# Mamba scan written feature by token in one set of matmuls, with the conv features and gates kept in memory chunk by chunk, in a hybrid decoder layer on Trainium2

## The reference, cut to what matters

```python
cum = jnp.cumsum(dtc * a.reshape(g, r), axis=2)
seg = cum[:, :, :, None] - cum[:, :, None, :]
decay = jnp.exp(jnp.where(causal, seg, -jnp.inf))
cb = jnp.einsum('bcign,bcjgn->bcijg', cc, bc)
y_diag = jnp.einsum('bcijgr,bcjgrp->bcigrp', cb[..., None] * decay * dtc[:, :, None], xc)
to_end = jnp.exp(cum[:, :, -1:] - cum) * dtc
states = jnp.einsum('bcjgn,bcjgr,bcjgrp->bcgrpn', bc, to_end, xc)
chunk_decay = jnp.exp(cum[:, :, -1])
...
y_off = jnp.einsum('bcign,bcigr,bcgrpn->bcigrp', cc, jnp.exp(cum), h_prev)
return (y_diag + y_off).reshape(b, s, nh, hp), h_last.reshape(b, nh, hp, D_STATE)
...
y = y + xs.astype(jnp.float32) * d_skip.astype(jnp.float32)[:, None]
y = y.reshape(b, t, D_SSM) * jax.nn.silu(z.astype(jnp.float32))
```

## Time and profile before

| | |
|---|---|
| median of 3 runs | 1902.06 us (1902.06 to 1903.03) |
| the profiled execution's own time | 1900.08 us |
| its span, first to last instruction | 1898.1 us |
| PE busy / DVE / ACT / POOL | 1825.6 / 1418.9 / 900.3 / 1066.2 us |
| mean granted TensorE clock | 0.990 |
| `weave` | about 330 to 789 us of the span |
| `mixers` | about 782 to 1003 us |

### The profile page before, as it was taken

How to read it: one execution, slowest core, us unless ns; L and a number is a source line. 1 busy time by engine, 2 the same in 40 slices (tenths; PEclk the granted TensorE clock), 3 DMA queues, 4 the chain that set the end, 5 groups by cost and what they waited for, 6 DMA issues and landing times.

```text
span 1898.1 us, 33584 instructions
## 1 busy us (share of the span) xinstructions
PE 1825.6 (96%) x12740; PEld 1686.7 (89%) x12740; DVE 1418.9 (75%) x1915; ACT 900.3 (47%) x1680; POOL 1066.2 (56%) x863
## 2 busy tenths in 40 slices
PE   8999999899999999999988999999999999999999
PEld 7999999888888889755557799999999998999999
DVE  5788840698888767589987564897777779787876
ACT  5334422677777778556642012343333344444442
POOL 4588740677756766334443222355555557787774
PEclk9999999999999999989999999999999999999999
DMA  4444442645455442789976524215334366434442
GB/s 175 149 156 176 183 148 75 159 117 124 101 134 120 125 124 90 253 304 322 321 244 214 190 97 186 91 45 205 147 125 165 148 230 254 159 137 147 148 136 92
DMA packets 139097, 309.31 MB, mean 163 GB/s; under 512 B 31659, under 2 KB 65323, under 8 KB 135228
## 3 DMA queue, kind: packets, MB, share of 16 engines
q1 hardware_dynamic: 115356, 271.15, 42.8%
q10 hardware_dynamic: 23584, 36.04, 5.6%
HBM read 222.42 MB, written 93.28 MB: 166 GB/s over the span
## 4 chain that ended last, share of the span: by engine, by line
PE 72%; DVE 13%; issue 6%; DMA 4%; ACT 3%; POOL 2%; SPq 0%; ACTq 0%; DVEq 0%; POOLq 0%
PE ff_ps L2742 32%; PE proj_ps L469 9%; PE dense_ps L1055 6%; PE wo_psa L2577 5%; PE proj_ps L552 3%; PE att_t_ps L1087 2%; PE wo_psb L2709 2%; DVE silu_half L1216 2%; DMA tmp_xbc<-silu_half 1%; PE wo_psa L2709 1%; PE att_s_ps L1073 1%; DVE att_p L1169 1%; PE att_s_ps L1074 1%; PE ssd_in L1773 1%; DVE sa_vlo L2108 1%
## 5 line engine op out<-in xcount | busy, mean ns | idle before, releaser
L2742 PE MATMUL ff_ps<-ff_set,ff_wring 128*128 128x264 f32 x5376 | 661.1, 285 | 11.1 <-DVE ff_set L3355 4.4
L2742 PEld LDWEIGHTS ff_ps<-ff_set,ff_wring 128*128 128x128 f32 x5376 | 658.0, 189 | 13.8 <-DVE ff_set L3355 5.3
L2411 POOL TENSOR_TENSOR ff_wring<-const,ff_wring 128x256 fp32r<-128x256 f32 (+1 forms) x192 | 211.9, 1107 | 148.0 <-ACT ff_wring L2908 147.9
L985 POOL TENSOR_SCALAR att_p<-att_p,att_rden 128x128 f32<-128x128 f32 (+6 forms) x112 | 197.0, 1768 | 117.1 <-DVE att_rden L1147 116.8
L2908 ACT ACTIVATE ff_wring<-const 128x256 fp32r<-128x256 f32 (+1 forms) x192 | 93.6, 489 | 220.4 <-PE ff_ps L2742 116.0
L3377 DVE TENSOR_TENSOR h<-h,ff_ps 128x528 f32<-128x528 f32 x192 | 133.2, 700 | 51.8 <-PE ff_ps L2742 47.2
L1282 ACT ACTIVATE att_pThi<-att_t_ps 128x512 fp32r<-128x512 f32 x192 | 93.2, 487 | 93.7 <-PE att_t_ps L1087 79.4
L1055 PE MATMUL dense_ps<-u_hi,w_hi 128*128 128x352 f32 x480 | 121.8, 335 | 4.7 <-POOL w_lo L254 2.1
L1169 DVE CUSTOM_DVE_ANT_0 att_p<-att_s_ps,att_bias 128x128 f32<-128x128 f32 (+7 forms) x128 | 94.9, 753 | 37.9 <-PE att_s_ps L1074 34.7
L1156 DVE TENSOR_TENSOR att_pTlo<-att_t_ps,att_pThi 128x512 fp32r<-128x512 f32 x192 | 104.5, 551 | 20.5 <-ACT att_pThi L1282 19.8
L1055 PE MATMUL dense_ps<-u_hi,w_lo 128*128 128x352 f32 x480 | 119.4, 330 | 0.0
(11 more groups left out here) (385 smaller groups left out, 4350.8 us busy)
## 6 DMA issues: line engine op xcount, KB each, us to landing
tmp_r_sets<-h SPq DMA_DIRECT2D x16, 1848.0 KB, 6.4
ff_setraw<-tmp_r_sets SPq DMA_DIRECT2D x56, 528.0 KB, 5.4
sa_k<-in_cache_k SPq DMA_DIRECT2D x32, 640.0 KB, 9.1
sa_v<-in_cache_v SPq DMA_DIRECT2D x40, 512.0 KB, 4.6
w_raw<-in_w_feat SPq DMA_DIRECT2D x36, 512.0 KB, 6.3
out_qk<-proj_out SPq DMA_DIRECT2D x16, 528.0 KB, 7.9
tmp_bias_rows<-tmp_table ACTq DMA_DIRECT2D x8, 1024.0 KB
att_bias<-tmp_bias_rows SPq DMA_DIRECT2D x16, 512.0 KB, 3.5
```

Of the source, the lines that this page charges most:

```text
L985: pool.tensor_scalar(slot(h, qt), slot(h, qt), rden[:, qt, :], None, ALU.mult).then_inc(normed, 1)
L2411: pool.tensor_tensor(w_set(n)[:, 1], operand(q, m), w_set(n)[:, 0].bitcast(F32), ALU.subtract).then_inc(fw_split, 1)
L2742: mm = pe.matmul(ff_ps[:, (b + g) * 512:(b + g) * 512 + HG], ws[:, wi, k, :], xs[:, xi, k, g * HG:(g + 1) * HG], start=(opens and k == 0 a ...
```

## The change

1. `store_feat` and `store_last` write the features and gates chunk by chunk: row 128·n + p of `xbc` now holds, for partition p, the 12 tiles' 128 tokens of chunk n (6 KB in a row); `z` likewise with 8 tiles (4 KB). A store of a tile is cut into pieces of 512 B for it (1024 of them), where it was a row of 4 KB for each partition. `load_chunk` and `load_z` read a whole row for each partition, where they gathered 512 B pieces. The samples' columns go to tensors of their own (`xbc_s`, `z_s`), with one more store for each z tile.
2. `inner` is written with x·dt as the weights (64 features of one head), two heads side by side in 64 output partitions each, and the decay matrix as the moving side, so that the result comes out feature by token. The carried state's part is added in the same PSUM tile: the weights are the state, the moving side is `grown` = exp(cum)·C. `off`, `scale_off`, `add_inner` and `turn_y` are gone; `add_skip` reads the product directly, from two PSUM tiles.
3. `grown` is made for each group by ACT (`grow_exp`, an exponential of 128x1024) and POOL (`grow`, a product of 128x1024). It is read from the rows of cum before `segment` overwrites them. The decay of the state is cut in two halves (`decay`). The squares have a buffer of their own (`ssd_sq`).
4. The order of all engines' lists in a pass is rewritten.

```diff
-                    act.dma_start(rows[:, 0:SEQ], half[:, 0:SEQ]).then_inc(feat_stored, 16)
+                    act.dma_start(by_chunk("xbc", d), chunked(half[:, 0:SEQ])).then_inc(feat_stored, 16)
...
-                sp.dma_start(xbc[j][:], dram["xbc"][:, cols].rearrange("(f p) t -> p f t", p=P)).then_inc(loaded[j], 16)
+                if n >= 3:
+                    sp.wait_ge(grown_made, 2 * (n - 2))
+                sp.dma_start(xbc[j][:].rearrange("p f t -> p (f t)"), dram["xbc"][n * P:(n + 1) * P, :]).then_inc(loaded[j], 16)
...
-                for h in range(8 * g, 8 * g + 8):
-                    if h % 4 == 0:
-                        pe.wait_ge(mix_made, 4 * n + h // 4 + 1)
-                    mm = pe.matmul(in_ps[:, (h % 8) * HD:(h % 8 + 1) * HD], mixm[n % 2][:, h, :],
-                                   xdt[:, h * HD:(h + 1) * HD], start=True, stop=True)
+                if n:
+                    pe.wait_ge(y_skipped, 2 * n + g - 1)
+                    pe.wait_ge(grown_made, 2 * n + g - 1)
+                    pe.wait_ge(state_summed, 2 * n + g - 1)
+                for f in range(4):
+                    if f % 2 == 0:
+                        pe.wait_ge(mix_made, 4 * n + 2 * g + f // 2 + 1)
...
+                    for r in range(2):
+                        mm = pe.matmul(out(r), xdt[:, cols(r)], mixm[n % 2][:, 8 * g + 2 * f + r, :], start=True, stop=(n == 0))
+                    if n:
+                        for r in range(2):
+                            mm = pe.matmul(out(r), state[:, cols(r)], grown[g][:, 2 * f + r, :], start=False, stop=True)
...
+            def grow(n, g):
+                pool.wait_ge(grown_exp, 2 * n + g - 1)
+                pool.wait_ge(loaded[n % 2], 16 * (n // 2 + 1))
+                pool.tensor_tensor(grown[g][:], grown[g][:],
+                                   xbc[n % 2][:, KD + 2 + g, :].unsqueeze(1).broadcast_to([P, NH // 2, P]),
+                                   ALU.mult).then_inc(grown_made, 1)
...
+            def grow_exp(n, g):
+                act.wait_ge(rows_loaded[n % 2], 16 * (n // 2 + 1))
+                if n >= 2:
+                    act.wait_ge(in_made, 2 * n + g - 1)
+                act.activation(grown[g][:], mixm[n % 2][:, 8 * g:8 * g + 8, :], ACT.Exp).then_inc(grown_exp, 1)
...
+                if n + 1 < NC:
+                    grow_exp(n + 1, 0)
+                    segment_next(n + 1, 0)
+                    segment_next(n + 1, 1)
                 if n:
                     exponent(n)
                     square(n - 1)
                     keep_probs(n)
```

More of the change, by code:

```diff
@@ L1726, in turn_x @@
                 mm.then_inc(x_turned, 1)
-            def turn_y(n, g):
-                pe.wait_ge(y_summed, 2 * n + g + 1)
-                if 2 * n + g:
-                    pe.wait_ge(y_skipped, 2 * n + g)
-                for f in range(4):
-                    mm = pe.transpose(y_ps[:, f * P:(f + 1) * P], y[n % 2][:, (4 * g + f) * P:(4 * g + f + 1) * P],
-                                      kit.c(C_IDENT, P))
-                mm.then_inc(y_turned, 1)
             def norm_sums(n):
@@ L1744, in norm_sums @@
                 mm.then_inc(normed, 1)
-            def off(n, g):
-                if g:
-                    pe.wait_ge(y_scaled, 2 * n - 1)
-                else:
-                    pe.wait_ge(state_summed, 2 * n)
-                pe.matmul(off_ps[:], xbc[n % 2][:, KD + 2 + g, :], state[:, half(g)], start=True,
-                          stop=True).then_inc(off_made, 1)
-            def states(n, g):
-                if g:
-                    pe.wait_ge(state_summed, 2 * n + 1)
-                else:
-                    if n:
-                        pe.wait_ge(y_scaled, 2 * n)
+            def states(n, g):
+                if 2 * n + g:
+                    pe.wait_ge(state_summed, 2 * n + g)
+                if g == 0:
                     pe.wait_ge(xw_made, n + 1)
@@ L1804, in _ @@
                 if n:
-                    off(n, 0)
-                    turn_y(n - 1, 0)
+                    inner(n, 0)
                     sample_scores(n, 0)
-                    off(n, 1)
                     sample_scores(n, 1)
@@ L1811, in _ @@
                     sample_scores(n, 2)
-                    turn_y(n - 1, 1)
                     sample_scores(n, 3)
-                states(n, 0)
-                inner(n, 0)
-                states(n, 1)
-                if n:
+                    states(n, 0)
+                    inner(n, 1)
+                    if n + 1 < NC:
+                        chunk_start(n + 1)
                     sample_turn(n)
-                inner(n, 1)
+                    states(n, 1)
+                else:
+                    states(n, 0)
+                    inner(n, 0)
+                    states(n, 1)
+                    inner(n, 1)
                 sample_values(n, 0)
-                if n + 1 < NC:
+                if n == 0:
                     chunk_start(n + 1)
-                else:
-                    norm_sums(n - 1)
                 sample_values(n, 1)
@@ L1827, in _ @@
                     turn_x(n + 1, 0)
-                else:
-                    turn_y(n, 0)
                 sample_values(n, 2)
@@ L1922, in _ @@
                     kit.clear(pool)
-            mixed.pool_tail = skip_x, sum_squares
+            mixed.sum_squares = sum_squares
         @block.scalar
@@ L2002, in _ @@
                 if n + 1 < NC:
+                    keep_b(n + 1)
                     cast_v(n, 3)
-                    keep_b(n + 1)
                     cast_v(n, 4)
-                    for q in range(4):
-                        segment(n + 1, q)
+                    grow_exp(n + 1, 1)
+                    segment_next(n + 1, 2)
+                    segment_next(n + 1, 3)
             mixed.act_tail = square, cast_v
@@ L2048, in weigh @@
                                   ALU.mult).then_inc(x_kept, 1)
-            def scale_off(n, g):
-                dve.wait_ge(off_made, 2 * n + g - 1)
-                if g == 0 and n >= 2:
-                    dve.wait_ge(y_turned, 2 * n - 2)
-                dve.tensor_tensor(heads(y[n % 2][:, half(g)]), heads(off_ps[:]), per_head(decays[:, 0, n, 8 * g:8 * g + 8]),
-                                  ALU.mult).then_inc(y_scaled, 1)
             def add_state(n, g):
@@ L2181, in _ @@
                     weigh(n + 1, 1)
-                    keep_own(n)
-                    scale_off(n + 1, 0)
                     mix(n + 1, 0)
@@ L2187, in _ @@
                         keep_norm(n - 1)
-            mixed.dve_tail = keep_own, add_skip, gate, keep_out, keep_norm, split_v
+                    keep_own(n)
+            mixed.dve_tail = keep_own, gate, keep_out, keep_norm, split_v
     return mixed
@@ L2616, in _ @@
                 step(k, (0, 1))
-                if k == 0:
-                    turn_y(last, 1)
                 if k == 1:
@@ L3090, in scale @@
                                          op1=ALU.mult).then_inc(y_scaled, 1)
-            keep_own, add_skip, gate, keep_out, keep_norm, split_v = mixed.dve_tail
+            keep_own, gate, keep_out, keep_norm, split_v = mixed.dve_tail
             last = mixed.chunks - 1
@@ L3098, in _ @@
             split_v(last, 4)
-            add_skip(last, 0)
             keep_own(last)
             split_a(2)
-            add_skip(last, 1)
             gate(last)
```

170 lines of the change are left out of this document (83 added, 87 removed).

## The result

The changed kernel took 1909.73 us (median of 5 runs, 1905.66 to 1911.8) against 1902.06 for the kernel before in the same job: ratio 1.0039, 95% interval 1.0025 to 1.0053. It is slower by 0.39%, about 7.5 us; the forecast was 1898, faster. Its profiled execution has a span of 1909.4 us (before 1898.1) and a mean granted clock of 0.986 (0.990).

What follows compares the result with a forecast made beforehand. Before, DVE was what a 23.74 us pass waits for most; after, late rows of cum would bind at 22.9. Terms -5.1 - 1.3 + 2.8 = -3.6 us from 1902.06 gave 1898.5, given as 1898; 8-in-10 range 1887 to 1910.

Steps and rivals of the forecast that it cites:

- -5.1 for the passes: Loop of `mixers`: six passes each 0.85 us shorter, at 22.9 us, set by late rows of cum; chance 0.32.
- -1.3 for the loop's end: End of the `mixers` loop: an `add_skip` of 0.69 us and a turn of 0.6 leave the chain.
- +2.8 for the stores: `weave`: feature stores in 512 B pieces land 0.7 us later, on the path about four times.
- further falls of the clock: Rival, loop of `mixers`: PE's clock falls more often, 3.5 us each; slower from the third, 1909; chance 0.17.
- dear stores: Rival, `weave`: stores cost their upper bound, 18 us; about 1911; chance 0.10, shared with `inner` products at 4.1 us.
- 10.2 + 3.8 = 14 us, in gaps that are there: POOL in a pass: two added products of 128x1024, 1.91 us each, fit into its idle time.
- DVE's 21.3: DVE's stretches of a pass, 10.66 + 4.45 + 6.18 us; the pass length if rows of cum land in time, chance 0.22.
- about 1.9 us of work: DVE in a pass: two mixes between the last `weigh` and `keep_own`, covering the wait for PE's last value product.
- The rows of cum: Loop from last value product through the rows' load, ACT and softmax to the next: 22.7 to 23.6 us, binding.
- ACT's 4.8: ACT in a pass: one exponential and half the next chunk's `segment` ahead of the softmax's exponentials, 4.8 us.
- A group of `inner` in 16 products: PE in a pass: 2.1 us a group if two products run side by side, 4.1 if not.
- The wait of DVE ahead of `keep_own`: DVE in a pass: its 1.32 us wait for PE's last value product vanishes.

Runs made afterwards that it cites:

- the rows in time: Changed kernel with the rows of cum issued right behind the features, ahead of the values: 1897.1 us, ratio 0.9982 to the kernel before.
- the memsets: Changed kernel, rows of cum loaded ahead of the values, three POOL memsets in place of each `grow` product, state's part left out: 1891.83 us, ratio 0.9954.
- the run with one head of eight: Changed kernel, rows of cum loaded ahead of the values, POOL's product with C made for only one head of eight: 1886.7 us, ratio 0.9935.
- The layout alone: Kernel before with the change's stores and loads of features and gates, and its old mixers: 1902.62 us, ratio 1.0024.
- the run with `skip_x` twice: Kernel before with POOL's product of the skip made twice in each chunk: 1926.45 us, ratio 1.0131.

## Why the prediction was wrong, point by point

The forecast was the sum -5.1 for the passes, -1.3 for the loop's end and +2.8 for the stores. The two profiled spans differ by +11.3: the five middle passes give +7.3 (125.69 us against 118.37), the rest of the loop -1.0, and `weave` +5.2; -0.2 lie behind the loop. The passes are where it failed. That 1909.73 still lies under the 1910 of the range is luck: that end stood for further falls of the clock or for dear stores, and not for a longer pass.

**"POOL gets two products [...] 10.2 + 3.8 = 14 us, in gaps that are there", and with it DVE's 21.3.** This is the step that failed: it priced each engine's list by itself, as if nothing that POOL does could lengthen an instruction of DVE. The gaps were there for POOL's time, but beside DVE's mixes and splits, with which POOL's products exclude each other. In the pass with the rows in time, mixes and splits wait 5.2 us: 2.77 and 2.98 for two pairs of mixes instead of 1.28 (as beside the memsets), and two splits at 2.14 and 2.31 instead of 1.22. Of this, 2.4 stand beside a `grow` (the mixes at 901.00 and the split at 915.53). The other 2.8 stand beside products that POOL made before the change too: the mixes at 921.04 beside `weigh_x`, where the prediction put "about 1.9 us of work" and 2.98 were measured, and the split at 918.20 beside `skip_x`. The kernel before had about 1.1 of such waits already, and showed it:

```profile
895.88 1.87 DVE L2016 TENSOR_TENSOR ssd_m<-ssd_m,ssd_cb 128x512 f32<-128x512 f32 x2
...
898.01 0.68 DVE L2016 TENSOR_TENSOR ssd_m<-ssd_m,ssd_cb 128x512 f32<-128x512 f32 x1
...
899.81 1.19 DVE L2016 TENSOR_TENSOR ssd_m<-ssd_m,ssd_cb 128x512 f32<-128x512 f32 x1
```

```profile
898.02 2.44 POOL L1912 TENSOR_TENSOR ssd_state<-ssd_state,ssd_decays 128x1024 f32<-128x1024 f32 x1 [0.82 <-POOL sa_bias L1863]
```

One mix 0.68, another 1.19, of the same size: the second ends 0.54 us after POOL's decay (898.02 + 2.44 + 0.54 = 901.00). The prediction took the mean of these (0.95 for a mix) as the price of the instruction. With 4.1 us more of waiting, not all of it on the path, 21.3 becomes the measured 24.5. By itself this already makes a pass 0.7 us longer than before. Taking most of the two products away gives back 1.6 of the 3.2 (22.87, the run with one head of eight).

**The rows of cum.** The mechanism was right and its size too small; in the kernel as built this loop is the longer one, so this term failed as well. From the last value product to the landing passed 8.3 us (904.34 to 912.64; forecast 6.1 to 7.0). The prediction took the landing down from the 8.2 us of the earlier trace rows, since the features no longer go ahead of it; it stayed at 7.7. ACT's 4.8 was right (912.66 to 917.53). From there to the split probabilities 3.4 (forecast 4.4). To the next last value product 8.7 (forecast 7.4), in which both the lock (split 2.32) and the fallen clock stand. Sum 25.2, where 22.7 to 23.6 was forecast. Even with the landing as forecast, DVE's 24.5 would have bound.

**PE.** A group of `inner` in 16 products took 1.97 us (forecast 2.1), and PE's work in a pass at full clock 20.1 (forecast 19.4):

```profile
914.64 0.44 PE L1775 MATMUL ssd_in<-ssd_m,ssd_xdt 128*64 128x128 f32 x4
...
916.22 0.39 PE L1778 MATMUL ssd_in<-ssd_grown,ssd_state 128*64 128x128 f32 x4
```

The wait of DVE ahead of `keep_own` is gone, as forecast.

**The clock.** In two of five middle passes the clock fell behind the wait that the rival named (late exponentials), but longer waits at the same place passed without a fall, so what decides is open. Nor did it fall in every pass, as in the loop of the section that the prediction quotes. A fall cost little here: the passes with one take 24.75 and 25.25, those without 24.64 to 25.54, since the load and DVE decide. In the run with `skip_x` twice, where PE and DVE are the bound, 0.83 instead of 0.94 went with 4 us more in a pass.

**The stores.** Forecast 2.8 us, with 5 us or more of waits at the samples' store: 6.4 measured. The stores themselves land 5.4 us after issue instead of 3.3. The softmax of the first sample starts at 797.2 us on average with the new layout (six profiles, 793.6 to 799.4) and at 794.3 with the old one (eight, 793.4 to 795.8): 2.9 later, with a scatter as large. The layout alone measures +4.6 us (+1.3 to +7.8) by the ratio; with the new mixers the old layout gives back 8.4 us when the rows are late and 1.5 when they are early. The sign is right, and the size is not resolved.
The Trainium skill, page "DMA: Bandwidth & Descriptors", section "Specifications", whose 512 B would have made these stores free, is not borne out for them: DVE's wait behind them is 4.6 to 6.4 us in the six profiles with the new layout, and 0.2 to 2.5 in the eight with the old one.

**The loop's ends.** From the first load of the rows to the output projection passed 233.8 us (787.79 to 1021.63) against 227.5 (782.55 to 1010.06): 6.3 longer. The five middle passes alone are 7.3 longer, so start and end together gained 1.0; the forecast had 1.3. The rest of the 11.3 us between the two spans, 5, lies ahead of the mixers, in `weave`.

What stays open: how the 12.6 us of the early rows (between medians of two jobs) divide. Between the two profiled spans lie 8.3. The five passes give 0.67 each, 3.3; the first one took 28.05 us at a granted clock of 0.88 in the changed kernel and 24.83 at 1.00 with the rows early, 3.2; another 2.2 lie in `weave`, which the early rows don't touch.

## What to carry to other kernels

A product of two SBUF operands given to GpSimd was free here only where VectorE, at the same moment, worked on something with at most one operand in SBUF; look at what lies beside the gap, not at its length. The same holds when nothing is added: a new order that puts such an instruction of VectorE beside an old product of GpSimd costs as much. When instructions of one size have two durations in a trace, find out what runs beside the long ones before taking the mean as a price. And a load whose buffer is free early belongs ahead of loads that wait for the last work of the pass.

## What the runs showed of the hardware

- VectorE with two operands in SBUF and GpSimd reading two operands in SBUF exclude each other by whole instructions, in both directions: a mix 0.6 to 0.7 us alone and up to 2.3 behind GpSimd (kernel before, `skip_x` twice); a split 1.22 and up to 2.95; GpSimd's `skip_x` and `weigh_x` 1.90 alone and 2.28 to 2.92. `grow`, of the same size, takes 2.4 alone and 2.81. Beside memsets of GpSimd, or with one operand in PSUM, VectorE's instructions keep their time.
- One product of 1.9 us more on an idle GpSimd gave VectorE 2.5 to 3.1 us more of busy time in a pass, and the pass 2.9 to 6.9 us, with the fallen clock.
- Reading the features in rows of 6 KB instead of 512 B pieces took the DMA share of 860 to 955 us from 0.95 to 0.89 in the layout run. The features landed 5.7 us after issue instead of 6.1, but no pass got shorter, as no load stands in the chain of those passes.
- The granted clock fell from 1.00 to 0.50 in two passes of the changed kernel, in which PE waits 1.03 and 1.47 us for the late exponentials, and stayed at 1.00 in two others, in which it waits 1.76 us.
